# The SSM part of an input projection, by token blocks: the first in float32, the other two in three rounded passes

## The reference

```python
h = rmsnorm(x, g_mix) * (1 + scale_m) + shift_m
proj = h @ w_in                                     # 512 u, 512 v, 512 ub columns
a_out, v_rows = gmlp_mix(proj[..., :2 * GMLP_WIDTH], v_gain, w_s, b_s)
ub = proj[..., 2 * GMLP_WIDTH:].reshape(bt, seq_len, SSM_GROUPS, SSM_GROUP).astype(F32)
y_ssm, h_re, h_im = s5_mix(ub, h0_re, h0_im, a_re, a_im, log_dt, b_re, b_im, c_re, c_im, d_skip)
```

## Time and profile before

| | |
|---|---|
| median of 3 runs | 969.5 us (969.48 to 973.18) |
| profiled execution | 975.78 us, span 973.4 us |
| mean granted TensorE clock | 0.983 |
| busy: PE, PE weight loads | 923.8 us (95%), 725.9 us (75%) |
| busy: DVE, ACT, POOL | 689.0 (71%), 449.0 (46%), 145.2 (15%) |

### The profile page before, as it was taken

One profiled execution on the slowest core, in us unless ns is written; L12 is line 12 of the kernel. 1 busy time (PEld: TensorE's weight loads), 2 busy tenths in 40 slices (PEclk: granted clock), 3 DMA queues, 4 the chain that ended last, 5 costly groups with the idle time before them and its releaser, 6 DMA issues.

```text
span 973.4 us, 14799 instructions
## 1 busy us (share of the span) xinstructions
PE 923.8 (95%) x5147; PEld 725.9 (75%) x5147; DVE 689.0 (71%) x1232; ACT 449.0 (46%) x744; POOL 145.2 (15%) x188
## 2 busy tenths in 40 slices
PE   3799999999999999999889999999999999999995
PEld 3465688566667878886369899999998889989742
DVE  4489433788583655555878778888887879879658
ACT  6442132511113632224336366666666576666553
POOL 7000000333230230000021011111102011111240
PEclk9889999999999999999989999999999999999998
DMA  9920299255447799916247788888889799789676
GB/s 297 384 95 28 62 159 84 87 186 197 158 154 264 283 206 226 261 57 229 118 129 233 230 291 281 266 268 264 260 289 329 281 303 335 270 292 340 225 246 248
DMA packets 122109, 216.88 MB, mean 223 GB/s; under 512 B 11988, under 2 KB 70048, under 8 KB 122040
## 3 DMA queue, kind: packets, MB, share of 16 engines
q1 hardware_dynamic: 103288, 155.17, 49.9%
q0 software_dynamic: 11360, 36.89, 14.0%
q10 hardware_dynamic: 7408, 24.13, 6.7%
HBM read 174.14 MB, written 40.80 MB: 221 GB/s over the span
## 4 chain that ended last, share of the span: by engine, by line
PE 81%; DVE 6%; DMA 6%; SPq 2%; issue 2%; ACT 2%; ACTq 0%; POOL 0%; DVEq 0%; POOLq 0%
PE bank L1318 13%; PE bank L1324 8%; PE bank L1054 6%; PE bank L1319 6%; PE bank L1088 5%; PE bank L1340 4%; PE bank L1247 4%; DVE arena L1448 3%; PE bank L1249 3%; PE bank L1248 3%; PE bank L1187 3%; DMA arena<-in_w_ada_dram 3%; PE bank L1403 2%; PE bank L1404 2%; PE bank L981 2%
## 5 line engine op out<-in xcount | busy, mean ns | idle before, releaser
L1448 DVE TENSOR_TENSOR w_lo<-w_raw,w_hi 128x1024 fp32r<-128x1024 f32 x192 | 227.4, 1221 | 36.7 <-ACT w_hi L824 34.6
L1318 PE MATMUL bank<-x_hl,w_hi 128*128 128x320 f32 (+2 forms) x768 | 216.5, 359 | 2.5 <-DVE arena L1891 2.5
L824 ACT CAST w_hi<-w_raw 128x1024 fp32r<-128x1024 f32 x192 | 191.1, 1052 | 32.4 <-DVE arena L1448 19.3
L1319 PE MATMUL bank<-x_hl,w_lo 128*128 128x160 f32 (+2 forms) x768 | 189.7, 247 | 0.0
L1318 PEld LDWEIGHTS bank<-x_hl,w_hi 128*128 128x128 f32 x768 | 145.4, 189 | 6.9 <-DVE arena L1891 3.0
L1319 PEld LDWEIGHTS bank<-x_hl,w_lo 128*128 128x128 f32 x768 | 147.5, 192 | 0.9 <-issue 0.4
L1448 DVE TENSOR_TENSOR arena<-arena 128x512 f32<-128x512 f32 (+14 forms) x250 | 122.5, 493 | 23.8 <-ACT arena L790 15.6
L1448 DVE TENSOR_TENSOR arena<-bank,arena 128x512 f32<-128x512 f32 (+4 forms) x60 | 38.5, 667 | 46.7 <-PE bank L1249 32.6
L1088 PE MATMUL bank<-arena 128*128 128x384 f32 x192 | 64.4, 490 | 1.1 <-ACT arena L722 1.1
L1054 PE MATMUL bank<-arena 128*128 128x384 f32 x192 | 62.1, 486 | 0.0
L1247 PE MATMUL bank<-wo_hi,m_hi 128*128 128x512 f32 x144 | 56.9, 395 | 0.6 <-issue 0.6
(11 more groups left out here) (355 smaller groups left out, 1642.0 us busy)
## 6 DMA issues: line engine op xcount, KB each, us to landing
w_raw<-in_w_gate_dram SPq DMA_DIRECT2D x64, 512.0 KB, 6.4
w_raw<-in_w_up_dram SPq DMA_DIRECT2D x64, 512.0 KB, 5.3
w_raw<-in_w_down_dram SPq DMA_DIRECT2D x64, 512.0 KB, 4.3
arena<-in_w_ada_dram SPq DMA_DIRECT2D x12, 2048.0 KB, 8.6
expert_rows<-arena POOLq DMA_DIRECT2D x1, 8704.0 KB, 48.7
expert_rows<-arena ACTq DMA_DIRECT2D x13, 512.0 KB, 7.0
h_scratch<-arena ACTq DMA_DIRECT2D x9, 512.0 KB, 6.9
out_dram<-arena SPq DMA_DIRECT2D x9, 512.0 KB, 4.7
```

Of the source, the lines that this page charges most:

```text
L824: a.copy(w_hi[n], w_raw[n]).then_inc(S["hi_done"], 1)
L1318: T.matmul(both, w_h, x, start=first, stop=False)
L1319: return T.matmul(o[:, 0:n], w_l, x_hl[:, k, 0, 0:n], start=False, stop=last)
L1448: return v.tensor_tensor(o, a, b, op)
```

## The change

The SSM projection runs by token blocks: `tb, j = divmod(n, 4)`. Token block 0 (outputs 0 to 3) stays in float32. Blocks 1 and 2 (outputs 4 to 11) take three rounded passes, 24 matmuls an output. ScalarE makes the high parts, GpSimd the low ones. The low weights are written over the raw weights, so the low part of block j waits until TensorE has done output j. The stores of `ub` become one for each output (192 KB, runs of 48 floats), from six buffers. The casts of the v weights move from outputs 0 to 3 to outputs 8 to 11 (`wv_hi` shares region RB with the new low columns). On VectorE the low v weights move from before the E table to places in and behind it, and E waits for `ub_ps` 8 in place of `ada_used` 1, since the high columns of block 1 lie where E is written. The memset of MT moves behind the low parts on GpSimd (`wu_hi` lies there), and SP waits for `zeroed` 6. Some semaphores are shared with the output projection under new names, with their counts shifted.

```diff
@@ GpSimd
+            def ub_columns_low(tb, half):
+                gp.wait_ge(S["cols_hi"], 2 * tb - 1 + half)
+                ks = slice(4 * half, 4 * half + 4)
+                g.tensor_tensor(hb_lo_halves[tb, half][:, :, :], hT[:, ks, 384 * tb:384 * tb + 384], hb_hi[tb][:, ks],
+                                ALU.subtract).then_inc(S["cols_lo"], 1)
+
+            def ub_weights_low(j):
+                gp.wait_ge(S["w_hi_done"], j + 1)
+                gp.wait_ge(S["ub_ps"], j + 1)
+                sl = slice(P * j, P * j + P)
+                g.tensor_tensor(wu_lo[:, :, sl], wu_raw[:, :, sl], wu_hi[:, :, sl], ALU.subtract).then_inc(S["w_lo_done"], 1)
+            ub_columns_low(1, 0)
+            ub_weights_low(0)
+            ub_columns_low(1, 1)
+            for j in range(1, KG):
+                ub_weights_low(j)
+            ub_columns_low(2, 0)
+            ub_columns_low(2, 1)
+            gp.wait_ge(S["ub_ps"], 12)
+            g.memset(MT, 0.0).then_inc(S["zeroed"], 1)
@@ ScalarE
+            act.wait_ge(S["ht_sb_v"], 2)
+            act.wait_ge(S["ht_sb_s"], 2)
+            ub_columns_high(1, 0)
+            arrived(act, ("in", 2))
+            ub_weights_high(0)
             for n in range(12):
-                j, tb = divmod(n, 3)
+                tb, j = divmod(n, KG)
                 act.wait_ge(S["ub_ps"], n + 1)
...
+                if n >= 6:
+                    act.wait_ge(S[f"ub_out{n % 2}"], 16 * (n // 2))
+                a.copy(ubT[:, n % 6], B[4 + n % 4][:, 0:384].rearrange("p (c s) -> p s c", s=L)).then_inc(S["ub_sb"], 1)
+                act.wait_ge(S["ub_sb"], n + 1)
+                act.dma_start(ub_d[P * j:P * j + P, :, 48 * tb:48 * tb + 48], ubT[:, n % 6]).then_inc(S[f"ub_out{n % 2}"], 16)
+                if n == 0:
+                    ub_columns_high(1, 1)
+                    ub_weights_high(1)
+                if n == 1:
+                    ub_weights_high(2)
+                    ub_weights_high(3)
+                if n == 2:
+                    act.wait_ge(S["ht_sb_v"], 4)
+                    act.wait_ge(S["ht_sb_s"], 3)
+                    ub_columns_high(2, 0)
+                    ub_columns_high(2, 1)
...
+                if 8 <= n:
+                    if n == 8:
+                        arrived(act, ("in", 1))
+                    v_weights_high(2 * (n - 8))
+                    v_weights_high(2 * (n - 8) + 1)
@@ TensorE
             for n in range(12):
+                tb, j = divmod(n, KG)
+                o = B[4 + n % 4][:, 0:384]
                 if n >= 4:
                     pe.wait_ge(S["ub_sb"], n - 3)
+                if tb == 1:
+                    pe.wait_ge(S["w_lo_done"], j + 1)
                 for k in range(KD):
+                    if tb == 0:
+                        last = T.matmul(o, wu_raw[:, k, P * j:P * j + P], hT[:, k, 0:384], start=(k == 0), stop=(k == KD - 1))
+                    else:
+                        if j == 0 and k % 4 == 0:
+                            pe.wait_ge(S["cols_lo"], 2 * tb - 1 + k // 4)
+                        w_h, w_l = wu_hi[:, k, P * j:P * j + P], wu_lo[:, k, P * j:P * j + P]
+                        h_h, h_l = hb_hi[tb][:, k], hb_lo_halves[tb, k // 4][:, k % 4]
+                        T.matmul(o, w_h, h_h, start=(k == 0), stop=False)
+                        T.matmul(o, w_h, h_l, start=False, stop=False)
+                        last = T.matmul(o, w_l, h_h, start=False, stop=(k == KD - 1))
                 last.then_inc(S["ub_ps"], 1)
@@ VectorE
-            for k in range(KD):
+            def v_weights_low(k):
                 dve.wait_ge(S["wv_hi_done"], k + 1)
                 tt(wv_lo[:, k], wv_raw[:, k], wv_hi[:, k], ALU.subtract).then_inc(S["wv_lo_done"], 1)
...
             v_columns_low(0)
             v_columns_low(1)
-            dve.wait_ge(S["ada_used"], 1)
+            dve.wait_ge(S["ub_ps"], 8)
...
                 n *= 2
+                if n in (SS // 2, SS):
+                    for k in range(2) if n < SS else range(2, 5):
+                        v_weights_low(k)
+            for k in range(5, KD):
+                v_weights_low(k)
```

More of the change, by code:

```diff
@@ L109, in hybrid_step @@
         bT = area("RC", 0, KG, TOK)
-        ubT = area("RD", 0, 2, L, CH)
+        ubT = area("RD", 0, 6, L, CH // 3)
         U = area("RE", 0, SG, CH)
@@ L186, in hybrid_step @@
         b_lo = rounded("b_lo", "RC", 0, KG, TOK)
+        wu_raw, wu_lo = rounded("wu_raw", "RW", 4096, KD, 512, dt=F32), rounded("wu_lo", "RW", 4096, KD, 512)
+        wu_hi = rounded("wu_hi", "RG", 0, KD, 512)
+        hb_hi = {1: rounded("hb_hi1", "RW", 0, KD, 384), 2: rounded("hb_hi2", "RE", 0, KD, 384)}
+        hb_lo_halves = {(1, 0): rounded("hb_lo10", "RB", 0, 4, 384), (1, 1): rounded("hb_lo11", "RB", 1536, 4, 384),
+                        (2, 0): rounded("hb_lo20", "RE", 3072, 4, 384), (2, 1): rounded("hb_lo21", "RB", 3072, 4, 384)}
+        UB_HALVES = 4
         WO_PIECES = [(0, 0), (0, 2), (0, 4), (0, 6), (1, 4), (1, 6), (1, 0), (1, 2)]
@@ L267, in hybrid_step @@
                  "bc_sb wo_ps wo_used x1_done ss_done h2_rows h2_out0 h2_out1 h2t_ps h2t_sb lg_ps "
-                 "wv_hi_done wv_lo_done hmh_done hml_done wo_hi_done wo_lo_done mh_done ml_done "
+                 "wv_hi_done wv_lo_done hmh_done hml_done w_hi_done w_lo_done cols_hi cols_lo "
                  "place_done list_sb list_out tab_done idx_in rows_in xt2_ps xt2_sb gate_done "
@@ L369, in _ @@
             sp.wait_ge(S["ada_used"], 2)
-            load("in", 2)
+            load("in", 2, wu_raw[:, :, :])
             sp.wait_ge(S["ada_used"], 3)
@@ L376, in _ @@
             sp.wait_ge(S["tables"], 3)
-            sp.wait_ge(S["zeroed"], 1)
+            sp.wait_ge(S["zeroed"], 6)
             for s in range(L):
@@ L380, in _ @@
             sp.wait_ge(S["mt_placed"], 16 * L)
-            sp.wait_ge(S["ub_out0"], 16 * KG // 2)
-            sp.wait_ge(S["ub_out1"], 16 * KG // 2)
+            sp.wait_ge(S["ub_out0"], 16 * 6)
+            sp.wait_ge(S["ub_out1"], 16 * 6)
             for s in range(L):
@@ L480, in _ @@
             gp.dma_start(dqnat[0:SG], d_skip[0]).then_inc(S["ld_s5a"], 16)
-            g.memset(MT, 0.0).then_inc(S["zeroed"], 1)
             for r, (s_in, b_in) in enumerate(((state_re, b_re), (state_im, b_im))):
@@ L678, in v_columns_high, with ub_columns_high, ub_weights_high @@
                 a.copy(hm_hi[:, t % 2], hT[:, :, P * t:P * t + P]).then_inc(S["hmh_done"], 1)
+            def ub_columns_high(tb, half):
+                ks = slice(4 * half, 4 * half + 4)
+                a.copy(hb_hi[tb][:, ks], hT[:, ks, 384 * tb:384 * tb + 384]).then_inc(S["cols_hi"], 1)
+            def ub_weights_high(j):
+                sl = slice(P * j, P * j + P)
+                a.copy(wu_hi[:, :, sl], wu_raw[:, :, sl]).then_inc(S["w_hi_done"], 1)
+            act.wait_ge(S["ht_sb_v"], 2)
@@ L775, in wo_high @@
                 h, k = WO_PIECES[piece]
-                a.copy(wo_hi[h][:, k:k + 2], wo_raw[h][:, k:k + 2]).then_inc(S["wo_hi_done"], 1)
+                a.copy(wo_hi[h][:, k:k + 2], wo_raw[h][:, k:k + 2]).then_inc(S["w_hi_done"], 1)
             def m_high(t, part):
@@ L782, in m_high @@
                 src, at = (uT, 0) if part == 0 else (bT, KG)
-                a.copy(m_hi[:, t % 2, at:at + KG], src[:, :, P * t:P * t + P]).then_inc(S["mh_done"], 1)
+                a.copy(m_hi[:, t % 2, at:at + KG], src[:, :, P * t:P * t + P]).then_inc(S["cols_hi"], 1)
             for n in range(16):
@@ L1042, in _ @@
             pe.wait_ge(S["cond_t"], 4)
-            w = arrived(pe, ("in", 2))
+            arrived(pe, ("in", 2))
+            pe.wait_ge(S["ht_sb_v"], 1)
+            pe.wait_ge(S["ht_sb_s"], 1)
             for n in range(12):
[L1046 to L1050, removed]
+                tb, j = divmod(n, KG)
+                o = B[4 + n % 4][:, 0:384]
                 if n >= 4:
                     pe.wait_ge(S["ub_sb"], n - 3)
+                if tb == 1:
+                    pe.wait_ge(S["w_lo_done"], j + 1)
                 for k in range(KD):
-                    last = T.matmul(B[4 + n % 4][:, 0:384], w[:, k, P * j:P * j + P], hT[:, k, 384 * tb:384 * tb + 384],
-                                    start=(k == 0), stop=(k == KD - 1))
+                    if tb == 0:
[8 more added lines that the diff above has]
+                        last = T.matmul(o, w_l, h_h, start=False, stop=(k == KD - 1))
                 last.then_inc(S["ub_ps"], 1)
@@ L1240, in _ @@
                     if t == 0:
-                        pe.wait_ge(S["wo_lo_done"], 4 + 4 * h)
+                        pe.wait_ge(S["w_lo_done"], KG + 4 + 4 * h)
                     o = B[4 + n % 4][:, :]
@@ L1244, in _ @@
                         if h == 0 and k % KG == 0:
-                            pe.wait_ge(S["ml_done"], 2 * t + k // KG + 1)
+                            pe.wait_ge(S["cols_lo"], UB_HALVES + 2 * t + k // KG + 1)
```

(10 more changed lines are left out.)

1 line of the change is left out of this document (removed).

## The result

The changed kernel takes 977.85 us (median; 975.67 to 978.75) against 969.5 beside it on the same chip: ratio 1.0073, 95% interval 1.0055 to 1.0092. It is slower, by 7.1 us by this ratio; the two medians are 8.4 apart. The forecast was 979, range 961 to 986.

What follows compares the result with a forecast made beforehand. TensorE bounds the stretch, but VectorE's low v weights, delayed 21 us by GpSimd's reads, would come after it: v 5.9 us later plus 3.4 of slow clock, +9.3 on 969.5, say 979, range 961 to 986.

Steps and rivals of the forecast that it cites:

- TensorE: In the SSM projection, 64 float32 products become 192 rounded matmuls at 0.174 us: 8.0 us saved, between 2.9 and 10.6.
- ScalarE: Casts of high parts beside the projection stay under 5.2 us an output; v casts, the last to 110.5, cost nothing.
- GpSimd: Eight subtractions between 59.7 and 86 us, about 3.8 and 2.6 each, 25.6 in all; TensorE doesn't wait for them.
- VectorE's loss: From 59.7 us on, GpSimd's SBUF reads take 21 us from VectorE; bounds 18.0 and 28.8, 23.4 taken, less 2.4.
- The way behind it: VectorE from `ub_ps` 8 to v: 23.6 us of work; with the loss ready at 129.8, v 5.9 us later.
- The clock: After 14 us idle before v, TensorE runs at the 1.2 GHz level: 3.4 us lost.
- The sum: +5.9 for v's later start and +3.4 for the slow clock: +9.3 us on the median 969.5, say 979.
- The stores: Twelve `ub` stores of 192 KB, 4.1 us each against 4.17 an output, just keep up.
- Rival 1: VectorE between 59.7 and 86 loses no more than 7 us to GpSimd: 963, between 960 and 966; chance 0.24.
- Rival 3: VectorE keeps the port, GpSimd loses; TensorE waits at outputs 4 and 8, v starts near 132; chance 0.08.
- Rival 2: VectorE loses 9 to 15 us, or rounded matmuls take 0.20: gain and wait cancel, 966 to 974; chance 0.10.

Runs made afterwards that it cites:

- kernel 3: The changed kernel with all eight `wv_lo` ahead of table E, E waiting for `ub_ps` 12 and its work area moved; 966.8 us, ratio 0.9969.
- kernel 9: As kernel 5, but the eight low halves made by VectorE instead of GpSimd; 963.5 us, ratio 0.9939.
- kernel 5: As kernel 3, with low columns of v tile 2 before E's last doubling and of tile 3 inside it; 962.69 us, ratio 0.9909.
- kernel 7: The changed kernel with each of GpSimd's eight subtractions cut in four (384 or 256 elements); 976.22 us, ratio 1.0055.
- kernel 8: The changed kernel with GpSimd's eight subtractions replaced by one-input copies of the same size, leaving wrong values; 983.11 us, ratio 1.0129.
- kernel 6: The changed kernel with thirty unused short TensorE matmuls filling most of the wait before v; 978.45 us, ratio 1.0073.
- kernel 2: The changed kernel with the eight low halves made by VectorE, behind its short instructions, instead of GpSimd; 970.03 us, ratio 0.9994.
- kernel 1: The changed kernel with GpSimd's eight subtractions replaced by memsets of the same tiles, low halves zero; 962.94 us, ratio 0.9934.
- kernel 4: The kernel before the change, plus eight GpSimd subtractions of the same sizes with unused results; 971.09 us, ratio 1.0003.

## Why the prediction was right, step by step
- **TensorE.** Right. The rounded outputs come 4.16 us apart (29.12 us between the copies at 76.18 and 105.30, seven steps), 0.1733 a matmul against 0.174 taken; not 0.20. v could have started 61.2 after the projection's first matmul (kernels 3 and 9); the steps said 61.0, and the earlier trace rows have 69.1.
- **ScalarE.** Right: no wait of TensorE names its casts. Once they did set VectorE's last `wv_lo` pair, 1.6 us in kernel 5, under cover.
- **GpSimd.** 3.46 and 2.36 us instead of 3.8 and 2.6, 23.2 for the eight instead of 25.6. The two sizes give 2.15 ns an element and 0.16 us fixed, where the forecast had 2.42 ns, from a 256-element instruction, and 0.1. The Trainium skill (GPSIMD Engine Reference, section Elementwise, side by side) has 2.6 cycles an element, and the trace agrees: 2.15 ns are 2.58 cycles at 1.2 GHz. By that figure alone the eight would be an estimated 22.2 us; the 23.5 of the prediction doesn't follow from it.
- **VectorE's loss.** 21 predicted, 45.6 - 24.3 = 21.3 measured. The mechanism was the forecast's: the held instructions stand 2 to 3.5 us each, one at a time behind whole GpSimd instructions. The closeness is partly luck. The 23.4 that it starts from is the middle of 18.0 and 28.8, and neither bound is GpSimd's time as the prediction itself has it, 25.6; by its own mechanism that gives 25.6 - 2.4 = 23.2. Two errors cancelled: GpSimd took only 23.2, and 1.9 of it was no loss, about what the eight held instructions take by themselves. The hold for a whole instruction agrees with the Trainium skill (SBUF — State Buffer, Who interferes with whom); kernels 7 and 8 add that long VectorE instructions hold GpSimd off just so. `W` ended at 101.6, which is 104.3 in the front of the earlier trace rows, against "near 105".
- **The way behind it.** From E's start to v's start 23.6 us forecast, 23.65 measured (103.98 to 127.63). v starts 76.5 after the projection's first matmul, the forecast being 75.0. One microsecond of the difference is the front: the projection followed ScalarE's first activation by 2.7 us here and 3.6 before.
- **The clock.** A term that was too dear: 3.4 predicted, 1.4 measured (V 49.8 against 48.4, and kernel 6). I had read the stretch of the earlier trace rows, four slices below 2.4 GHz, and had written that an idle time of 14 us can't come cheaper. Here 15.3 us did: the granted clock was 0.50 to 130 and 0.85 in the next slice, so back at about 130.6, 3 us after v's start instead of 7, and half of them lost. It had fallen near 117, while TensorE was idle. The price doesn't go by the length of the idle time: V is 1.5 over before in kernel 2 (5.2 us idle) and 2.9 in kernel 7 (7.7 us idle, clock back after 6 us). What sets it no run here tells, so 1.4 replaces 3.4 for this kernel only.
- **The sum.** v starts 7.4 later by D, where the forecast had 5.9, and the clock took 1.4 instead of 3.4: the errors of 1.5 and 2.0 have opposite signs, and that they cancel is luck. The traces make it +8.8, the forecast +9.3, and measured are +7.1 to +8.4 (by the ratio, and by the difference of the medians).
- **The stores.** Right that they don't bind: 2.7 us to landing at the median, below the 4.1 that I took from the placing into MT, and no wait of ScalarE's names them. Their issue costs 0.52 instead of 0.35 each.
- **The rivals.** Rival 1 named the right time for its condition and the condition was false: kernel 1 has it, at 962.9. Rival 3 didn't happen, since GpSimd met only short instructions; its mechanism, TensorE at output 8 waiting for `cols_lo`, is seen in kernel 7. Rival 2 needed a loss of 9 to 15; kernel 2, with 11.2, is where it lies: 970.0.

What stays open: the start of the projection differs by up to 4.6 us between executions of equal code. In the trace of before the granted clock was 0.50 from 44 to 52 us and 0.56 to 54, just ahead of the projection, and in that of after 1.00 all that time; why one execution has the low clock there and another doesn't, no run here tells.

## What to carry to other kernels
Work given to an idle GpSimd is paid by VectorE where both read SBUF. Here each GpSimd instruction held one VectorE instruction for nearly its whole length: 23.2 us of GpSimd took 21.3 us, nearly twice the 11.7 that VectorE would have needed for the same work. Count the cover before the engine: the 34 us by which the low halves of v were ready early would have paid for the whole loss, as kernel 4 shows, until the same change also put 19 us of other work ahead of it. When a change is slower, look for that second edit first; moving E behind the weights, with the low columns of v placed to suit, turned +7 us into -9, and GpSimd kept its work.

## What was not expected of the hardware
- Short and long instructions meet by one rule, and it is the lengths that make the price. Beside instructions of 16 to 64 elements GpSimd lost next to nothing (3.46 us for 1536 elements) and VectorE waited; beside those of 2304 elements in kernel 7 they took turns, one instruction each, and both slowed (GpSimd's 384 elements from 0.97 to 3.3 us, VectorE's from 2.57 to 3.27).
- One tensor input doesn't keep a VectorE instruction clear of it: the TENSOR_SCALAR of 16 elements took 2.25 us instead of 0.17.
- A copy by GpSimd, with one input, holds VectorE off as well; a memset doesn't (W 24.3, as without it).
- A wait of 3.4 us inside a busy stretch was followed by 4 us of granted clock 0.50 to 0.68 (kernel 3), and V was 5.3 longer. The 15.3 us idle before v cost only 1.4 on top, and 7.7 us idle in kernel 7 cost 2.9.
- A store in 1024 pieces of 192 B landed in 2.7 us.
